# A two-part transformer block with an RWKV-7 chunk loop: b, k and v turned in another way, the block inverse's gather in pieces, GpSimd's order changed

## The chip, the cores and the metric

The kernel runs on one core of one Trainium2 chip, in one launch. The metric is device time in microseconds (us). Five engines work side by side, each through its own list of instructions, in order: TensorE (PE; its weight loads are shown as PEld), VectorE (DVE), ScalarE (ACT), GpSimd (POOL) and SyncE (SP), which here issues transfers. They wait for each other by semaphores only. TensorE writes to PSUM, eight banks of 128 x 512 float32.

## The reference

First two attention blocks with feed-forward parts on 512 tokens of width 1024; then one RWKV-7 block whose core is a recurrence over time for each of 16 heads of width 64, with a state S of 64 x 64:

```python
def step(S, inp):
    r_t, w_t, k_t, v_t, a_t, b_t = inp
    sa = jnp.einsum('bhvk,bhk->bhv', S, a_t)
    S = S * w_t[:, :, None, :] + sa[..., None] * b_t[:, :, None, :] + v_t[..., None] * k_t[:, :, None, :]
    y = jnp.einsum('bhvk,bhk->bhv', S, r_t)
    return S, y
```

Then a norm over each head, a gate, a convolution branch, an output projection and a last feed-forward part. All of it is float32.

## The kernel before

Most of the time goes into projections in which each float32 product is taken as three of rounded halves (lines 2351 to 2353). The change lies in the **chunk loop** between the projections "z" and "rwkv_out". There the recurrence is cut into eight chunks of 64 tokens, taken as four **pairs** j = 0 to 3. Inside a chunk the 64 steps become matrix products that hold the inverse of a triangular 64 x 64 matrix for each head.

The order of the loop is one list, `products` (lines 514 to 533). Each entry is a group of TensorE products with a kind and an index; TensorE, VectorE and ScalarE each walk the list and do what the kind asks. A product takes one of four slots of two PSUM banks in turn (`slot_of`), so TensorE's product m waits until the copies of product m - 4 have been made. Kinds:
- **lab**: b against kk, masked by VectorE into `wk["lab"]`; GpSimd later adds the unit diagonal ("eye", line 964).
- **z, turn, tri, triT**: two levels (4 and 5) that extend the inverse of the 16 x 16 diagonal blocks to 64 x 64. VectorE masks z; ScalarE copies turn and triT. The first level reads `wk["tri"]`, filled by `spread_blocks` (line 599).
- **pairs**: products of b and k with r and kk, masked by VectorE. **v**: v centred and turned, tokens on the partitions. **lv**: its product with `wk["lak"]`.
- **x, u, ys** of chunk i: state against kk; the solve; the output (part 0) and the new state (part 1, which VectorE adds and decays, lines 2192 and 2193).
- **bk** (j, cb) for each chunk cb of pair j: b and k turned so that tokens lie on the partitions, b of the chunk in one half of the 128 partitions and k in the other. One half can be written by a transpose, the other by a product with the identity. ScalarE copies each bank in one go (line 1516). `wk["bk"]` has one buffer for each cb; ys of the state reads it.
- **sums, rows, bonus, rstd**: sums for the head norm.

The inverse of the 16 x 16 blocks works on two pairs at once (a **batch**). `blocks_of` gathers the blocks of both pairs by four operations over 128 x 512 (line 2112), each taking the one before as an input, and turns them (line 2120). `block_inverse` makes 28 small steps, `blocks_back` turns the result into `wk["inv"]` (line 2125), and `spread_blocks` writes a pair's blocks to `wk["tri"]`. Batch 0 (pairs 0 and 1) is VectorE's from gather to spread of pair 0, right behind the masks of lab 1; VectorE masks lab 2 and 3 behind it. Batch 1 (pairs 2 and 3) is gathered by VectorE behind the last pairs mask of pair 0, inverted by GpSimd, and turned back by VectorE behind the last z mask of pair 1. GpSimd's order is: the eyes of lab 0 to 3, those of 2 and 3 only when batch 1 has been gathered, since the gather wants the matrices without them; the inverse of batch 1; the spreads of pairs 1, 2 and 3.

SyncE's queue reloads `u_b` (line 741) with stored activations when the last pairs product and bk (3, 0) are out, then `u_kk` when x 7 is out, then more when ys 7 is.

Of the kernel before, what the change touches and what calls it, by code (L numbers as in the profile page):

```python
# [5 lines left out]
P = 128  # L6
D = 1024
KD = D // P
# [9 lines left out]
C = 64  # L18
# [98 lines left out]
def build(nc, t, out, scratch):  # L117
# [4 lines left out]
    with ctx:  # L122
# [593 lines left out]
        def _(sp):  # L716
# [3 lines left out]
            for p, pan in enumerate(panels):  # L720
# [14 lines left out]
                if p == L["rwkv_out"].p0 + 6:  # L735
# [3 lines left out]
                    product_out(sp, "bk", (NC // 2 - 1, 0))  # L739
# [73 lines left out]
        def _(pool):  # L813
# [186 lines left out]
        def _(act):  # L1000
# [482 lines left out]
            for m, (kind, i) in enumerate(products):  # L1483
                slot = slot_of(m)
                for part in parts_of((kind, i)):
# [22 lines left out]
                    if kind == "v":  # L1508
                        written(act, product, part)
                        for cb in range(2):  # L1510
                            ins = nc.scalar.activation(wk["uv"][side(1 - cb), i % 2, cb, 8 * part:8 * part + 8, :],
                                                       src[side(1 - cb)], ACT.Copy)
                        ins.then_inc(bank_out[bank], 1)
                    if kind == "bk":
                        written(act, product, part)
                        nc.scalar.activation(wk["bk"][:, i[1], 8 * part:8 * part + 8, :], src, ACT.Copy
                                             ).then_inc(bank_out[bank], 1)
# [48 lines left out]
        def _(dve):  # L1566
# [537 lines left out]
            def blocks_of(batch):  # L2104
# [3 lines left out]
                added = masks[:, M_BLOCKS, BS:2 * BS].unsqueeze(1).broadcast_to([P, 2 * RH, BS])  # L2108
                for j in (2 * batch, 2 * batch + 1):
                    product_out(dve, "lab", j)  # L2110
                for q in range(NB):
                    ins = nc.vector.scalar_tensor_tensor(by_row, lab[:, :, q * BS:q * BS + BS], masks[:, M_BLOCKS, q:q + 1],
                                                         added, ALU.mult, ALU.add)
                    if q == NB - 1:
                        ins.then_inc(sg["blocks_read"], 1)
                        dve.wait_ge(sg["blocks_read"], batch + 1)
                    else:
                        link(ins)
                    added = by_row
# [10 lines left out]
            for m, (kind, i) in enumerate(products):  # L2130
                slot = slot_of(m)
                for part in parts_of((kind, i)):
# [3 lines left out]
                    if kind == "lab":  # L2136
# [4 lines left out]
                        if i % 2 and part:  # L2141
                            batch = i // 2
                            if batch == 0:
                                blocks_of(batch)
# [4 lines left out]
                    elif kind == "pairs":  # L2149
# [8 lines left out]
                        if i == (0, 1, 1):  # L2158
                            blocks_of(1)
                    elif kind == "z":  # L2160
# [5 lines left out]
                        if i == (1, LEVELS[1], 1):  # L2166
                            dve.wait_ge(sg["blocks_inverted"], 1)
                            blocks_back(1)
# [21 lines left out]
                    elif kind == "ys" and part == 1:  # L2190
# [3 lines left out]
                                                ALU.mult).then_inc(bank_out[bank], 1)  # L2194

# [81 lines left out]
        def _(pe):  # L2277
# [515 lines left out]
            for m, (kind, i) in enumerate(products):  # L2793
# [23 lines left out]
                elif kind == "v":  # L2817
                    for c in range(KD):
                        dst = ps[:, banks[c // 4], c % 4 * P:(c % 4 + 1) * P]
                        for cb in range(2):  # L2820
                            last = nc.tensor.matmul(dst[side(1 - cb)], u_v[:, c, tokens(i, cb)],
                                                    masks[:, M_CENTER:M_BLOCKS, :].rearrange("p a n -> p (a n)"),
                                                    start=True, stop=True)
                        if c % 4 == 3:
                            last.then_inc(sg["product_done"], 1)
                elif kind == "bk":
                    for c in range(KD):
                        dst = ps[:, banks[c // 4], c % 4 * P:(c % 4 + 1) * P]
# [92 lines left out]
                elif kind == "ys":  # L2921
# [14 lines left out]
                    if 1 in parts_of((kind, i)):  # L2936
                        product_out(pe, "bk", (j, cb))
# [121 lines left out]
```

## Time and profile before

| | us |
|---|---|
| median of 3 timed runs (2365.84 to 2371.52) | 2366.89 |
| the profiled execution | 2364.72 |
| its span, first to last instruction | 2362.8 |
| TensorE busy | 2268.7 (96%) |
| VectorE, ScalarE, GpSimd busy | 1015.0, 875.9, 1024.4 |
| the chunk loop, first lab to last ys on TensorE | 1684.2 to 1856.8 |

Mean granted clock of TensorE over the span: 0.982. In a timeline a row gives start, duration, engine, line, operation, what it writes and reads, the count of instructions merged, and in brackets how long the engine stood idle before it and what ended that. A float32 product counts twice there (two passes), a transpose once. In a table of windows a row gives the stretch and its length, then for each engine its busy time and count, then the granted clock of TensorE as a share of 2.4 GHz (PEclk), the share of the DMA engines and GB/s.

### The profile page before, as it was taken

To read this page: it belongs to the slowest core of one execution; us is meant where nothing else is said; L and a number is where in the kernel's file an instruction comes from. 1 tells how busy PE (TensorE), PEld (TensorE's weight loads), DVE (VectorE), ACT (ScalarE), POOL (GpSimd) and SP (SyncE) were. 2 spreads that over 40 slices of the span, in tenths; PEclk is the share of its full clock that TensorE was granted. 3 is DMA by queue.
4 is the path that set the end of the run, shared out by engine and by line. 5 is a ranking of instruction groups with operands and counts; after the bars stand their busy time and mean duration, and the time that the engine had idled before them with its cause. 6 is when DMAs were issued, how large, how long until landed. Compare 5 with 4: busy or idle time off the path is not lost.

```text
span 2362.8 us, 36049 instructions
## 1 busy us (share of the span) xinstructions
PE 2268.7 (96%) x14668; PEld 1859.4 (79%) x14668; DVE 1015.0 (43%) x1655; ACT 875.9 (37%) x1488; POOL 1024.4 (43%) x605
## 2 busy tenths in 40 slices
PE   7999999999999999999999999999879999999998
PEld 6867888888986688888877888777667778888888
DVE  6264522211456553222125988626843555322212
ACT  5264523322414563332234223353424345333222
POOL 4423544444542264444454444434330465544443
PEclk9999999999999999999999999999979999999999
DMA  6601333333442023333333333322100522333332
GB/s 173 150 23 39 98 106 97 98 96 93 98 119 58 10 72 99 98 98 102 98 86 112 98 99 98 116 94 72 50 3 3 179 77 85 98 99 98 93 98 69
DMA packets 386294, 209.87 MB, mean 89 GB/s; under 512 B 36927, under 2 KB 378663, under 8 KB 385875
## 3 DMA queue, kind: packets, MB, share of 16 engines
q1 hardware_dynamic: 383011, 196.68, 29.4%
q0 software_dynamic: 2448, 9.70, 1.1%
q8 instruction: 119, 1.95, 0.4%
q10 hardware_dynamic: 672, 1.18, 0.1%
q14 instruction: 44, 0.36, 0.0%
HBM read 196.65 MB, written 12.41 MB: 88 GB/s over the span
## 4 chain that ended last, share of the span: by engine, by line
PE 81%; POOL 7%; issue 6%; DVE 4%; ACT 2%; DMA 0%; ACTq 0%; POOLq 0%; DVEq 0%
PE ps L2351 23%; PE ps L2352 23%; PE ps L2353 23%; POOL w_lo L836 3%; PE ps L2561 2%; PE ps L2546 2%; PE ps L2536 2%; POOL x_res L903 1%; PE ps L2831 1%; PE ps L2524 1%; POOL u_b L933 0%; PE ps L2933 0%; PE ps L2885 0%; PE ps L2814 0%; PE ps L2424 0%
## 5 line engine op out<-in xcount | busy, mean ns | idle before, releaser
L836 POOL TENSOR_TENSOR w_lo<-raw,w_hi 128x1024 fp32r<-128x1024 f32 (+2 forms) x344 | 823.2, 2397 | 887.2 <-ACT w_hi L1025 882.2
L2351 PE MATMUL ps<-h_hi,w_hi 128*128 128x512 f32 (+1 forms) x2112 | 817.5, 387 | 20.5 <-DVE h_lo L1712 4.5
L2352 PE MATMUL ps<-h_hi,w_lo 128*128 128x512 f32 (+1 forms) x2112 | 805.3, 381 | 0.0
L2353 PE MATMUL ps<-h_lo,w_hi 128*128 128x512 f32 (+1 forms) x2112 | 805.2, 381 | 0.0
L1025 ACT ACTIVATE w_hi<-raw 128x1024 fp32r<-128x1024 f32 (+1 forms) x344 | 358.6, 1043 | 1113.4 <-PE ps L2353 1101.7
L2351 PEld LDWEIGHTS ps<-h_hi,w_hi 128*128 128x128 f32 x2112 | 399.3, 189 | 113.5 <-issue 31.7
L2353 PEld LDWEIGHTS ps<-h_lo,w_hi 128*128 128x128 f32 x2112 | 399.3, 189 | 77.1
L2352 PEld LDWEIGHTS ps<-h_hi,w_lo 128*128 128x128 f32 x2112 | 399.7, 189 | 74.7 <-issue 1.2
L2351 PE MATMUL ps<-hid_hi,w_hi 128*128 128x512 f32 (+1 forms) x616 | 221.8, 360 | 0.0
L2353 PE MATMUL ps<-hid_lo,w_hi 128*128 128x512 f32 (+1 forms) x616 | 220.9, 359 | 0.0
L2352 PE MATMUL ps<-hid_hi,w_lo 128*128 128x512 f32 (+1 forms) x616 | 220.9, 359 | 0.0
L1991 DVE SCALAR_TENSOR_TENSOR ps<-u_w,vecs,ps 128x511 f32<-128x511 f32 (+28 forms) x232 | 151.9, 735 | 0.0
L1776 DVE TENSOR_TENSOR hid<-ps,spread_s 128x512 f32<-128x512 f32 x66 | 45.6, 691 | 242.5 <-PE ps L2353 242.5
L1770 DVE TENSOR_TENSOR silu<-ps,spread_s 128x512 f32<-128x512 f32 x66 | 45.6, 691 | 229.3 <-PE ps L2353 229.2
L1594 DVE TENSOR_TENSOR h_sq<-h_sq 128x512 f32<-128x512 f32 x16 | 36.1, 2259 | 248.2 <-ACT h_sq L1130 157.0
L2352 PEld LDWEIGHTS ps<-hid_hi,w_lo 128*128 128x128 f32 x616 | 116.4, 189 | 17.2
L2353 PEld LDWEIGHTS ps<-hid_lo,w_hi 128*128 128x128 f32 x616 | 116.3, 189 | 17.3
L2351 PEld LDWEIGHTS ps<-hid_hi,w_hi 128*128 128x128 f32 x616 | 116.3, 189 | 17.1
L873 POOL TENSOR_TENSOR h_lo<-o_raw,h_hi 128x512 fp32r<-128x512 f32 x16 | 20.4, 1276 | 88.5 <-ACT h_hi L1240 88.5
L1260 ACT ACTIVATE score<-score,row_max 128x257 f32<-128x257 f32 (+3 forms) x96 | 49.7, 519 | 19.9 <-DVE row_max L1825 17.6
L1764 DVE TENSOR_TENSOR hid_lo<-hid,hid_hi 128x512 fp32r<-128x512 f32 x66 | 53.8, 816 | 2.9 <-ACT hid_hi L1203 2.6
L1203 ACT ACTIVATE hid_hi<-hid 128x512 fp32r<-128x512 f32 x66 | 41.9, 635 | 34.9 <-DVE hid L1780 34.9
(359 smaller groups left out, 2508.7 us busy)
## 6 DMA issues: line engine op xcount, KB each, us to landing
raw<-in_w_gu SPq DMA_DIRECT2D x88, 512.0 KB, 3.8
raw<-in_w_in SPq DMA_DIRECT2D x56, 512.0 KB, 3.9
raw<-in_w_down SPq DMA_DIRECT2D x32, 448.0 KB, 3.5
raw<-in_ffn_w_gate SPq DMA_DIRECT2D x22, 512.0 KB, 3.9
raw<-in_ffn_w_up SPq DMA_DIRECT2D x22, 512.0 KB, 3.8
raw<-in_w_in_b SPq DMA_DIRECT2D x20, 512.0 KB, 3.8
raw<-in_w_down SPq DMA_DIRECT2D x16, 512.0 KB, 3.8
raw<-in_w_out SPq DMA_DIRECT2D x16, 512.0 KB, 3.7
```

Of the source, the lines that this page charges most:

```text
L836: nc.gpsimd.tensor_tensor(lo[:, k0:, :], src[:, k0:, :], hi[:, k0:, :].bitcast(f32), ALU.subtract).then_inc(lo_done, 1)
L1025: nc.scalar.activation(w_hi[split_slot[p]][:, k0:pan.kc, :], raw[:, raw_slot[p], k0:pan.kc, :], ACT.Copy).then_inc(hi_done, 1)
L1260: nc.scalar.activation(score[:, b, 0:w], score[:, b, 0:w], ACT.Exp, scale=-1.0, bias=row_max[:, b:b + 1], accum_out=total).then_inc(sg["ex ...
L1764: nc.vector.tensor_tensor(hid_lo[:, f, :], hid[:, f % 2, :], hid_hi[:, f, :].bitcast(f32), ALU.subtract).then_inc(sg["hid_lo_ready"], 1)
L1770: nc.vector.tensor_tensor(silu[:, f % 2, :], ps[:, g % 4, :], spread_s[:, :], ALU.mult).then_inc(bank_free[g % 4], 1)
L1991: nc.vector.scalar_tensor_tensor(u_kk[:, c, s:TOK] if last else acc[:, s:TOK], u_w[:, c, 0:TOK - s], tap(TAPS - 1 - s, c), acc[:, s:TOK], ...
L2351: nc.tensor.matmul(bank, wh[:, k, :], ah[:, part], start=first, stop=False)
L2352: nc.tensor.matmul(bank, wl[:, k, :], ah[:, part], start=False, stop=False)
L2353: return nc.tensor.matmul(bank, wh[:, k, :], al[:, part], start=False, stop=end)
L2536: nc.tensor.matmul(ps[:, i % 4, 0:u["w"]], u["q"], u["k"], start=True, stop=True).then_inc(sg["s_done"], 1)
L2546: last = nc.tensor.transpose(ps[0:m, 4 + k % 2, j * P:(j + 1) * P], score[:, k % SCORE_BUFFERS, off:off + m], ident[:, :])
L2561: ins = nc.tensor.matmul(ps[side(e), 6 + tile % 2, blk * P:(blk + 1) * P], v, pT[0:m, (k + e) % PT_BUFFERS, j * P:(j + 1) * P], start=(j = ...
```

## The change

1. **b and k.** The kinds bT j and kT j take the place of bk (j, cb). Each is eight whole 128 x 128 transposes, both chunks of the pair at once. In the result the tokens of each chunk fill one half of the partitions; ScalarE copies b straight and k into the other half of the partitions, each bank in two copies of 64 partitions. Pair 0 has both where the bk products were; for j > 0, bT, lv, kT stand behind the odd ys (and sums), none behind the even ys.
2. **v.** Products of 64 x 64 by the two diagonal blocks of the centring matrix, all heads of one parity to one bank.
3. **The gather of batch 1** is made in four pieces behind z (0, 5, 1), x 0 and z (1, 4, 0), from the matrices that have their eyes already, and turned behind z (1, 4, 1). `blocks_back(1)` stands behind ys 1.
4. **GpSimd** adds the eyes of lab 2 and 3 at once, and spreads pair 1 ahead of the inverse of batch 1.
5. SyncE's reload of `u_b` waits for bT 3.

```diff
-                products += [("lab", 0), ("lab", 1), ("v", 0), ("bk", (0, 0)), ("bk", (0, 1)), ("lab", 2), ("lab", 3)]
+                products += [("lab", 0), ("lab", 1), ("v", 0), ("bT", 0), ("kT", 0), ("lab", 2), ("lab", 3)]
...
-                products += [x0] + first + [u0] + pairs0 + middle + [ys0, ("bk", (j, 0))] + last + [x1] + pairs1 + [u1]
+                products += [x0] + first + [u0] + pairs0 + middle + [ys0] + last + [x1] + pairs1 + [u1]
...
-                products += [("bk", (j, 1))] if j < NC // 2 - 1 else []
-                products += [("lv", j)]
+                products += [("bT", j), ("lv", j), ("kT", j)]
...
-                    product_out(sp, "bk", (NC // 2 - 1, 0))
+                    product_out(sp, "bT", NC // 2 - 1)
...
                 product_out(pool, "lab", j)
-                pool.wait_ge(sg["blocks_read"], j // 2 + 1)
+                if j < 2:
+                    pool.wait_ge(sg["blocks_read"], 1)
...
-            pool.wait_ge(sg["blocks_turned"], 2)
-            block_inverse(nc.gpsimd, link).then_inc(sg["blocks_inverted"], 1)
             for j in range(1, NC // 2):
+                if j == 2:
+                    pool.wait_ge(sg["blocks_turned"], 2)
+                    block_inverse(nc.gpsimd, link).then_inc(sg["blocks_inverted"], 1)
                 pool.wait_ge(sg["blocks_back"], j // 2 + 1)
                 written(pool, ("turn", (j - 1, LEVELS[0], 1)))
                 spread_blocks(nc.gpsimd, j).then_inc(sg["tri_first"], 1)
...
+                            ins = nc.scalar.activation(wk["uv"][side(1 - cb), i % 2, cb, part::2, :], src[side(1 - cb)], ACT.Copy)
...
+                        for cb in range(2):
+                            to = side(cb if kind == "bT" else 1 - cb)
+                            ins = nc.scalar.activation(wk["bk"][to, cb, 8 * part:8 * part + 8, :], src[side(cb)], ACT.Copy)
...
+                    if batch:
+                        dve.wait_ge(sg["lab_eye"], 8)
+                        link(nc.vector.tensor_scalar(by_row, block, chosen, None, ALU.mult))
+                        return
...
+            def beside(product):
+
+                if product == ("z", (0, LEVELS[1], 1)):
+                    gather(1, 0)
+                    gather(1, 1)
+                if product == ("x", 0):
+                    gather(1, 2)
+                if product == ("z", (1, LEVELS[0], 0)):
+                    gather(1, 3)
+                if product == ("z", (1, LEVELS[0], 1)):
+                    turn_blocks(1)
+                if product == ("ys", 1):
+                    dve.wait_ge(sg["blocks_inverted"], 1)
+                    blocks_back(1)
...
                     for c in range(KD):
+                        for e in range(2):
+                            center = masks[side(e), M_CENTER + e, :]
+                            for cb in range(2):
+                                last = nc.tensor.matmul(ps[side(1 - cb), banks[e], c * C:(c + 1) * C],
+                                                        u_v[side(e), c, tokens(i, cb)], center, start=True, stop=True)
...
-                        for src, block in ((u_b, i[1]), (u_k, 1 - i[1])):
-                            turn = nc.tensor.matmul if block else nc.tensor.transpose
-                            last = turn(dst[side(block)], src[:, c, tokens(*i)], ident[:, :])
+                        both = (u_b if kind == "bT" else u_k)[:, c, 2 * i * C:(2 * i + 2) * C]
+                        last = nc.tensor.transpose(ps[:, banks[c // 4], c % 4 * P:(c % 4 + 1) * P], both, ident[:, :])
```

ys of the state (part 1) waits for bT j and kT j where it waited for bk (j, cb).

## Rows read from the trace of the kernel before

**Rows 1.** The page's part 4: the chain that ended last, by engine.

```profile
PE 81%; POOL 7%; issue 6%; DVE 4%; ACT 2%; DMA 0%; ACTq 0%; POOLq 0%; DVEq 0%
```

**Rows 2.** Timeline of TensorE, chunk pairs 0 and 1.

```profile
1699.04 2.09 PE L2804 MATMUL ps<-u_rkk,u_b 64*64 64x64 f32 x128
...
1709.65 1.13 PE L2885 MATMUL ps<-wk_tri,wk_lab 64*64 64x64 f32 x32 [8.52 <-DVE wk_tri L599]
...
1721.17 0.46 PE L2897 MATMUL ps<-ident,wk_tri 64*128 64x64 f32 x8 [0.50 <-DVE wk_lak L2156]
...
1727.08 1.98 PE L2870 MATMUL ps<-wk_uv,wk_lak 64*64 64x64 f32 x64 [5.45 <-DVE wk_z L2163]
...
1728.85 3.52 PE L2918 MATMUL ps<-wk_triT,wk_z 64*64 64x64 f32 x62
...
1744.41 1.13 PE L2885 MATMUL ps<-wk_tri,wk_lab 64*64 64x64 f32 x32 [11.30 <-POOL wk_tri L599]
```

**Rows 3.** Timeline of VectorE, the same stretch and the masks behind.

```profile
1721.04 1.09 DVE L2112 SCALAR_TENSOR_TENSOR wk_cols<-wk_lab,masks 128x512 f32<-128x512 f32 x1
...
1722.17 3.39 DVE L2112 SCALAR_TENSOR_TENSOR wk_cols<-wk_lab,masks,wk_cols 128x512 f32<-128x512 f32 x3
...
1726.34 1.29 DVE L2163 TENSOR_TENSOR wk_z<-ps,masks 128x512 f32<-128x512 f32 x2
...
1762.73 1.14 DVE L2125 STREAM_TRANSPOSE wk_inv<-wk_rows 128x512 f32<-128x512 f32 x1
```

**Rows 4.** Timeline of GpSimd: eyes, first step of the inverse, spread.

```profile
1725.72 4.96 POOL L964 TENSOR_TENSOR wk_lab<-wk_lab,masks 128x512 f32<-128x512 f32 x4 [25.46 <-DVE wk_cols L2112]
...
1730.65 0.27 POOL L589 TENSOR_TENSOR step_of<-wk_rows 128x28 f32<-128x28 f32 x1
...
1742.38 1.89 POOL L599 TENSOR_TENSOR wk_tri<-wk_inv,masks 128x1024 f32<-128x1024 f32 x1
```

**Rows 5.** Windows; PE busy first, PEclk after the POOL column.

```profile
1715.60:1721.60 6.00, 5.43 (x224) 4.87 (x218) 5.88 (x10) 1.20 (x2) 0.00 (x0) 0.99 0.02 4
1727.10:1732.70 5.60, 5.60 (x150) 5.60 (x153) 0.52 (x1) 1.86 (x4) 5.21 (x9) 0.50 0.01 3
1744.40:1749.80 5.40, 5.39 (x122) 4.93 (x126) 1.38 (x2) 1.22 (x3) 0.00 (x0) 0.50 0.01 3
1749.80:1778.60 28.80, 28.75 (x767) 23.20 (x761) 11.59 (x17) 12.29 (x22) 1.89 (x1) 1.00 0.01 4
```

**Rows 6.** Timeline of TensorE, later pairs.

```profile
1755.60 0.30 PE L2831 MATMUL ps<-ident,u_b 128*64 128x128 f32 x1
...
1755.83 0.43 PE L2831 MATMUL ps<-ident,u_k 128*64 128x128 f32 x2
...
1760.34 0.69 PE L2885 MATMUL ps<-wk_tri,wk_lab 64*64 64x64 f32 x32
...
1765.57 2.07 PE L2918 MATMUL ps<-wk_triT,wk_z 64*64 64x64 f32 x62
...
1767.57 1.97 PE L2821 MATMUL ps<-masks,u_v 128*64 128x128 f32 x32
...
1806.88 1.95 PE L2965 MATMUL ps<-head_ones,u_k 128*128 128x2 f32 x16
```

**Rows 7.** Timeline of TensorE: the transposes of x_in.

```profile
35.81 3.86 PE L2650 MATMUL ps<-ident,x_in 128*128 128x128 f32 x32 [0.78 <-issue]
```

**Rows 8.** Window of line 2650 alone: PE, PEld, PEclk, DMA share, GB/s.

```profile
35.80:39.40 3.60, 3.59 (x32) 3.39 (x32) 1.00 0.62 134
```

**Rows 9.** Timeline of ScalarE: copies of v, a copy of bk.

```profile
1768.71 2.42 ACT L1511 ACTIVATE wk_uv<-ps 64x512 f32<-64x512 f32 x4 [0.43 <-PE ps L2821]
...
1774.90 0.60 ACT L1516 ACTIVATE wk_bk<-ps 128x512 f32<-128x512 f32 x1 [2.06 <-PE ps L2831]
```

**Rows 10.** Line 741, the reload of u_b.

```profile
L741 SPq DMA_DIRECT2D u_b<-scratch_conv x8: 432/435/1387, 1835.0 to 1840.1; - x8
DMA to landing us min/median/max: 4.3/5.7/6.4
```

More of the change, by code:

```diff
@@ L1510, in _ @@
                         for cb in range(2):
-                            ins = nc.scalar.activation(wk["uv"][side(1 - cb), i % 2, cb, 8 * part:8 * part + 8, :],
-                                                       src[side(1 - cb)], ACT.Copy)
+                            ins = nc.scalar.activation(wk["uv"][side(1 - cb), i % 2, cb, part::2, :], src[side(1 - cb)], ACT.Copy)
                         ins.then_inc(bank_out[bank], 1)
-                    if kind == "bk":
+                    if kind in ("bT", "kT"):
                         written(act, product, part)
-                        nc.scalar.activation(wk["bk"][:, i[1], 8 * part:8 * part + 8, :], src, ACT.Copy
-                                             ).then_inc(bank_out[bank], 1)
+                        for cb in range(2):
+                            to = side(cb if kind == "bT" else 1 - cb)
+                            ins = nc.scalar.activation(wk["bk"][to, cb, 8 * part:8 * part + 8, :], src[side(cb)], ACT.Copy)
+                        ins.then_inc(bank_out[bank], 1)
                     if kind == "lv":
@@ L2102, in mask4, with gather @@
                 return m.broadcast_to([m.shape[0], 2, 4, C])
-            def blocks_of(batch):
+            def gather(batch, q):
                 lab = wk["lab"][:, 2 * batch:2 * batch + 2, :, :].rearrange("p j h n -> p (j h) n")
                 by_row = wk["cols"][:, :, :, :].rearrange("p t j h -> p (j h) t")
[L2108 to L2119, printed above, removed]
+                block, chosen = lab[:, :, q * BS:q * BS + BS], masks[:, M_BLOCKS, q:q + 1]
+                if q == 0:
+                    for j in (2 * batch, 2 * batch + 1):
+                        product_out(dve, "lab", j)
+                    if batch:
+                        dve.wait_ge(sg["lab_eye"], 8)
+                        link(nc.vector.tensor_scalar(by_row, block, chosen, None, ALU.mult))
+                        return
+                added = by_row if q else masks[:, M_BLOCKS, BS:2 * BS].unsqueeze(1).broadcast_to([P, 2 * RH, BS])
+                ins = nc.vector.scalar_tensor_tensor(by_row, block, chosen, added, ALU.mult, ALU.add)
+                if q == NB - 1:
+                    ins.then_inc(sg["blocks_read"], 1)
+                    dve.wait_ge(sg["blocks_read"], batch + 1)
+                else:
+                    link(ins)
@@ L2120, in blocks_of, with turn_blocks @@
+            def turn_blocks(batch):
                 nc.vector.transpose(wk["rows"][:, :, :, :], wk["cols"][:, :, :, :]).then_inc(sg["blocks_turned"], 1)
                 dve.wait_ge(sg["blocks_turned"], batch + 1)
+            def beside(product):
[11 more added lines that the diff above has]
+                    blocks_back(1)
@@ L2143, in _ @@
                             if batch == 0:
-                                blocks_of(batch)
+                                for q in range(NB):
+                                    gather(batch, q)
+                                turn_blocks(batch)
                                 link(block_inverse(nc.vector, link))
@@ L2157, in _ @@
                                                 ).then_inc(bank_out[bank], 1)
-                        if i == (0, 1, 1):
-                            blocks_of(1)
                     elif kind == "z":
@@ L2165, in _ @@
                                                 mask(M_LOW + l - LEVELS[0], [P, 2, 4, C]), ALU.mult).then_inc(bank_out[bank], 1)
-                        if i == (1, LEVELS[1], 1):
-                            dve.wait_ge(sg["blocks_inverted"], 1)
-                            blocks_back(1)
                     elif kind == "tri" and i[1] == 0:
@@ L2194, in _ @@
                                                 ALU.mult).then_inc(bank_out[bank], 1)
+                beside((kind, i))
             def low_of_y(c):
@@ L2818, in _ @@
                     for c in range(KD):
[L2819 to L2826, printed above, removed]
+                        for e in range(2):
[3 more added lines that the diff above has]
+                                                        u_v[side(e), c, tokens(i, cb)], center, start=True, stop=True)
+                            if c == KD - 1:
+                                last.then_inc(sg["product_done"], 1)
+                elif kind in ("bT", "kT"):
                     for c in range(KD):
-                        dst = ps[:, banks[c // 4], c % 4 * P:(c % 4 + 1) * P]
-                        for src, block in ((u_b, i[1]), (u_k, 1 - i[1])):
-                            turn = nc.tensor.matmul if block else nc.tensor.transpose
-                            last = turn(dst[side(block)], src[:, c, tokens(*i)], ident[:, :])
+                        both = (u_b if kind == "bT" else u_k)[:, c, 2 * i * C:(2 * i + 2) * C]
+                        last = nc.tensor.transpose(ps[:, banks[c // 4], c % 4 * P:(c % 4 + 1) * P], both, ident[:, :])
                         if c % 4 == 3:
@@ L2936, in _ @@
                     if 1 in parts_of((kind, i)):
-                        product_out(pe, "bk", (j, cb))
+                        product_out(pe, "bT", j)
+                        product_out(pe, "kT", j)
                         for h in range(RH):
```

## The prediction

> **What bounds the kernel now.** I began with the page: the span is 2362.8 us, and TensorE has 81% of the chain of work that ended last [rows 1]. So what the change is worth is what it takes from TensorE's line inside the chunk loop, and only the places count at which TensorE waits or is itself late. Second came the timeline of TensorE through the loop, read for the brackets of idle time [rows 2]. There are three large ones. At 1709.65 it has waited 8.52 us for VectorE's first wk_tri, at 1727.08 5.45 us for VectorE's z, and at 1744.41 11.30 us for GpSimd's wk_tri. Third, the timelines of the two engines named. VectorE stands in `blocks_of(1)`, four gathers (1.09 + 3.39) and a transpose, from 1721.04, and only at 1726.34 masks the z for which TensorE waits [rows 3]. GpSimd adds the eyes of chunk pairs 2 and 3 only after that gather (4.96 us from 1725.72), then runs the 28 steps of the block inverse from 1730.65 to 1742.4, and only then, for 1.89 us, spreads the blocks of pair 1, which it had in hand all the time (they come from batch 0) [rows 4]. Fourth, the same stretch in windows: the granted clock is 0.99 while TensorE works in 1715.6 to 1721.6, and 0.50 in the 5.6 us of work that follow its stand; it is 0.50 again in the 5.4 us after the long wait, and 1.00 for the 28.8 us behind that, in which TensorE is busy for 28.75 [rows 5]. So from 1755 on no wait is left: TensorE's own products are the time, and there every product taken away counts in full until another engine is late.
>
> **The change part by part.**
> *The first wait (8.52 us) stays.* It ends with VectorE's own inverse of batch 0, whose gathers, transposes and steps are as before. The shorter v and the transposes that stand before it only lengthen TensorE's idle time. So z of pair 0 starts at 1709.65 as before. Value 0; it could move by some tenths only if the masks of lab 0 and 1 moved, which nothing here touches.
>
> *The second wait (5.45) goes.* With the gather out of the way, VectorE masks z right behind the last pairs mask, at 1721.1; a mask takes 0.69, of which 0.6 up to the next start. lv of pair 0 needs the bank of the first z, so it starts at about 1721.85 in place of 1727.08: 5.2 us. What is late next is nothing of VectorE's: gather pieces 0 and 1 (2 x 1.1) stand behind the z masks, from 1722.4 to 1724.6, and x 0 reaches VectorE later than that.
>
> *The third wait (11.30) goes.* POOL's order is now eyes 0 and 1, eyes 2 and 3, spread 1, inverse, spread 2. Lab 2 and 3 are out at 1711.9, so the eyes end near 1716; spread 1 needs the last turn of pair 0, which ends at 1721.6 [rows 2], and is done 1.89 later, at 1723.6. x 0 ends at 1725.6 (next term), so z of pair 1 doesn't wait: 11.3 us. The inverse (11.75 us with its steps' gaps [rows 4]) starts when VectorE has turned the blocks, at about 1731, and ends near 1743; VectorE asks for it after the state update of ys 1, near 1750. It has 7 us to spare.
>
> *The clock between them.* lv and triT of pair 0 took 1.98 and 3.52 us at the half clock (1.2 GHz) [rows 2]; triT takes 2.07 at the full one (2.4 GHz) [rows 6], a factor of 1.7, by which lv takes 1.2: 2.3 us. TensorE no longer stands before them, so I take the full clock; the low end is 0. Behind the long wait TensorE worked 5.4 us at 0.50 [rows 5]; a z took 1.13 us there [rows 2] and 0.69 at the full clock [rows 6], a factor of 1.6, so this becomes 3.3: another 2.1 us.
>
> *bk by whole transposes.* Before, one bk product took 4.7 us from its first start to the next product (1755.60 to 1760.34; the other in the pair is its mirror image): per 128 columns a transpose of 64 tokens (0.23 us to the next start) and a plain product of two passes (the other 0.36 of 0.59) [rows 6]. There is no whole transpose in the loop; the nearest row is the 32 of x_in, 128 x 128 each, all of whose starts lie within 3.60 us at granted clock 1.00: 0.113 us each [rows 7, 8]. A bT or kT product is eight of them, 0.9 us. Bounds: 0.9 by that row, 1.8 if each went at the pace of the 64-token transpose in the loop (0.23); I take 0.9, since it is the same form. Pairs 1 and 2 had two bk products and get two short ones: 9.4 - 1.8 = 7.6 us each. Pair 3 had one bk and gets two short ones: 2.9. Pair 0 lies before the first wait: 0. Sum 18.1 us.
>
> *v by 64x64 products.* 1.97 us busy before, 1.9 to the next start [rows 6]. The new form (32 products in four quadrants, 64 moving columns) is that of lab, of which two went in 2.09 us [rows 2]: 1.0. Three v products count (pairs 1 to 3): 2.7 us.
>
> *What is added.* Gross this makes 5.2 + 11.3 + 2.3 + 2.1 + 18.1 + 2.7 = 41.7 us. Against it stand new waits, since three engines now have less time for the same copies.
> (a) Pair 1: VectorE has gather pieces 2 and 3 (2 x 1.1) and the turn (0.7) between x 0 and the masks of the pairs. Placed one by one behind x 0 (ends 1726.3), they push the last pairs mask from about 1731.5 to 1733.3, and ys 0 behind it: 1.8 us.
> (b) Behind each ys of odd number now stand bT, lv and kT on TensorE, 0.9 + 1.2 + 0.9. ScalarE must copy 4 + 2 + 4 times, where it copied 2 + 2; a copy over 64 partitions costs as much as one over 128 (4 in 2.42 us, against 0.60 for one) [rows 9]. The PSUM bank pair of a product is taken again four products later, so the second z of the next pair waits for kT's copies. Before pair 2: kT is out 6.4 us behind the end of ys, TensorE would be there at 5.0, and z waits 0.9 before that for the spread that comes behind `blocks_back` (two operations on the state, each as long as a mask, 1.4; blocks_back 1.1 [rows 3]; spread 1.89 [rows 4]): together 1.6 us. Before pair 3 there is also sums (1.95 us on TensorE [rows 6], two copies): kT is out at 8.4, TensorE there at 6.8: 1.6 us. In the tail the second sums waits 0.4 in the same way.
> The copies of kT cross from one half of the partitions to the other, and no row shows such a copy on ScalarE: between 0.60, as in [rows 9], and twice that. I take 0.60; at 1.2 the waits grow by 2.4 us at each of three places, 7 us.
> (c) The reload of u_b on SP's queue waits for bT 3 in place of bk (3, 0), so it starts near the end of pair 3 and not at 1835. Its eight pieces are issued in 5.1 us and each lands within 6.4 of its issue [rows 10]; the next transfer in the queue waits for x 7, 11 us later. It stays hidden; without that cover it would cost up to its 12 us.
> New waits 1.8 + 1.6 + 1.6 + 0.4 = 5.4. In these TensorE stands up to 1.6 us at a place, and before, it lost the full clock after standing; for one such fall I put in what the first one cost, 2.3 us. Net 41.7 - 5.4 - 2.3 = 34.0 us.
>
> The profiled execution took 2364.72 us (span 2362.8 and 1.9 around it), so the sum says 2330.7. The median of the three timed runs is 2.2 above the profiled one; the forecast for the median is 2333 us.
>
> **The rivals.**
> *The clock falls at every joint.* Behind ys now come sums, two products of nothing but transposes and a wait, where bk had kept TensorE going for 4.7 us. For it speaks that the clock was 0.50 after each stand in [rows 5]; against it, that 32 whole transposes in a row ran at 1.00 [rows 7, 8]. Work from bT to the second turn is 5.8 us at the full clock and 9.9 at the half one (factor 1.7), but the wait of 1.6 is then covered: 2.5 us; u, pairs and tri behind it cost 2 more. At three joints 13 us, gain 21 to 23: 2344 us.
> The Trainium skill, in "TensorE: Matmul & The Clock Gate", Part 4 (PE-mode transpose), says that the full clock does not engage for transposes. By it this rival would be the likely one; the x_in transposes, 0.113 us apart at granted clock 1.00, do not agree with it.
> *No new waits.* ScalarE's and VectorE's copies overlap better than I stack them. In [rows 9] two 64-partition copies never started less than 0.6 apart, which speaks against. Gain 41: 2326 us.
> *Copies across the halves are slow:* 1.2 us each, gain 27: 2340 us.
> *The waits only move.* The inverse on GpSimd runs beside a busy VectorE now, where before VectorE had nothing to do, and VectorE is blocked in order behind `blocks_inverted`. It decides from an inverse of 19 us (now 11.75); at 35 us the gain is down to 18: 2349 us. Against it: two of VectorE's masks took 1.29 us right beside GpSimd's adds, and those kept to 1.24 each [rows 3, 4].
> *Slower.* The clock stays at 1.2 GHz from 1722 to the end of the loop: dense small products and transposes do not bring it back as bk did. Some 100 us of TensorE work remain there, at 1.6 to 1.7 times the time: +60, against 36 gained: 2390 us. It decides from some 55 us of the loop at the half clock. Against it: between 1749.8 and 1778.6 the same small products ran at 1.00, bk being 9.4 of the 28.8 us [rows 5].
>
> **How the numbers follow.** Forecast (gain 28 to 38) 0.60; clock at every joint 0.17; no new waits 0.08; slow copies 0.08; waits only moved 0.04; slower 0.03. Range: from 2324 (all of 41.7 and a little) to 2346 (the clock rival and a little). Less than 0.3%, 7 us, cannot be told from no change in this kernel; half of the moved-waits case lies there. Faster 0.95, the same 0.02, slower 0.03.
>
> **What would show it.** TensorE starts lv of pair 0 near 1722, and z of pair 1 near 1726 without a wait for wk_tri. bT and kT are 8 transposes each, 0.9 us a product; v 1.0 us. ScalarE's copies behind odd ys are ten or twelve in a row, and the second z of pairs 2 and 3 waits for them. x 2 ends about 27 us earlier than 1778.8, the loop about 34 to 36 us earlier. The prediction is wrong if the granted clock of the loop is below 0.8 over long stretches, if VectorE waits for `blocks_inverted`, if a whole transpose takes more than 0.2 us, or if ScalarE becomes the engine that never waits in the loop.

## The result, and the profile after

| | before | after |
|---|---|---|
| median of the timed runs, us | 2366.98 (4 runs) | 2335.44 (2332.80 to 2337.06, 4 runs) |
| the profiled execution, its span, us | 2364.72, 2362.8 | 2332.80, 2331.0 |
| mean granted clock of TensorE | 0.982 | 0.986 |

The ratio is 0.9862, interval 0.9845 to 0.9879. The forecast was 2333 (2324 to 2346). In the page, TensorE's share of the chain that ended last is as before; GpSimd's has fallen by 1% of the span, and "issue" has grown by 1% [rows 1]:

```profile
PE 81%; issue 7%; POOL 6%; DVE 4%; ACT 2%; DMA 0%; ACTq 0%; POOLq 0%; DVEq 0%
```

To see where the time went I cut the loop where a product starts on TensorE. Each column runs from one such start to the next ("z 0" is the first z of pair 0, "z 1" that of pair 1). The last column ends at the last start among those products of ys 7 that read the state (1863.82 before, 1833.55 after), so this loop is longer than the one that the table of the kernel before gives (to 1856.8):

| us | lab 0 to z 0 | to lv 0 | to z 1 | to x 2 | to x 4 | to x 6 | to ys 7 | loop |
|---|---|---|---|---|---|---|---|---|
| before | 25.42 | 17.43 | 17.33 | 33.73 | 36.33 | 32.33 | 17.02 | 179.58 |
| after | 25.38 | 12.11 | 4.74 | 27.55 | 30.76 | 31.58 | 18.42 | 150.52 |
| taken away | 0.0 | 5.3 | 12.6 | 6.2 | 5.6 | 0.8 | -1.4 | 29.1 |
| by the prediction | 0 | 5.2 | 13.6 | 8.8 | 6.9 | 2.2 | -0.4 | 36.3 |

The last line is the prediction's own terms put in their places, without its 2.3 us for a fall of the clock that had no place. Between the two profiled executions lie 31.9 us: 29.1 in the loop, 1.2 in an earlier start of it, 1.6 behind it. Those 2.9 us are in no step. The loop starts at 1682.4 to 1690.6 in executions whose instructions are the same up to there, so single executions are compared below by the loop alone. The loop varies too: a second profiled execution of the changed kernel (h_after, below) has 151.60 us in place of 150.52.

TensorE's timeline of the changed kernel; [rows 2, 6] have the same products of before:

```profile
1708.40 1.13 PE L2904 MATMUL ps<-wk_tri,wk_lab 64*64 64x64 f32 x32 [16.22 <-DVE wk_tri L598]
...
1720.52 1.16 PE L2889 MATMUL ps<-wk_uv,wk_lak 64*64 64x64 f32 x64
...
1723.66 1.29 PE L2937 MATMUL ps<-wk_triT,wk_z 64*64 64x64 f32 x30 [1.05 <-issue]
...
1725.31 0.66 PE L2904 MATMUL ps<-wk_tri,wk_lab 64*64 64x64 f32 x30
...
1749.66 1.09 PE L2850 MATMUL ps<-ident,u_b 128*128 128x128 f32 x8
1750.68 1.16 PE L2889 MATMUL ps<-wk_uv,wk_lak 64*64 64x64 f32 x64
1751.78 1.09 PE L2850 MATMUL ps<-ident,u_k 128*128 128x128 f32 x8
...
1754.36 0.69 PE L2904 MATMUL ps<-wk_tri,wk_lab 64*64 64x64 f32 x32 [0.86 <-POOL wk_tri L598]
...
1756.42 0.69 PE L2904 MATMUL ps<-wk_tri,wk_lab 64*64 64x64 f32 x32 [0.97 <-issue]
...
1787.17 0.69 PE L2904 MATMUL ps<-wk_tri,wk_lab 64*64 64x64 f32 x32 [1.97 <-issue]
```

The reader is to see four things. The first wait ends where it did, with more idle time in it. The waits of 5.45 and 11.30 us are gone. Eight whole transposes stand where a bk product of 4.7 us did. And new small waits stand before the first z of pair 2 (the spread) and the second z of pairs 2 and 3, where "issue" hides ScalarE, whose copies fill the time without a gap:

```profile
1750.35 2.42 ACT L1518 ACTIVATE wk_bk<-ps 64x512 f32<-64x512 f32 x4 [0.42 <-PE ps L2850]
1752.80 1.08 ACT L1522 ACTIVATE wk_xx<-ps 128x512 f32<-128x512 f32 x2
1753.90 2.42 ACT L1518 ACTIVATE wk_bk<-ps 64x512 f32<-64x512 f32 x4
```

The last of these copies ends at 1756.32, and the second z starts at 1756.42. Windows of the changed kernel, columns as in [rows 5]: from the first z, over pairs 0 and 1, and the tail.

```profile
1708.40:1714.40 6.00, 6.00 (x137) 5.53 (x138) 4.13 (x7) 1.19 (x2) 4.80 (x4) 0.50 0.01 3
1714.40:1752.80 38.40, 33.19 (x1231) 30.31 (x1226) 25.90 (x36) 17.32 (x31) 12.72 (x31) 1.00 0.02 5
...
1815.10:1833.50 18.40, 17.53 (x293) 15.01 (x294) 7.78 (x14) 7.82 (x18) 7.29 (x5) 0.81 0.48 154
```

After the first wait the clock is at 0.50 (1.2 GHz) for 6 us as before, and then it holds 1.00 through three pairs. But in the second window TensorE is busy for only 33.19 of 38.40 us, although the timeline shows one wait for a semaphore in it, of 0.50 us. Seven rows with idle time and no releaser (0.33 to 1.05 us, two of them in the fences here: 1723.66 and 1746.87) make up 4.4 of the other 4.7. That gap is the part that the prediction had no term for, although the trace of before has such rows too, between 1778 and 1840 us:

```profile
1781.09 0.57 PE L2885 MATMUL ps<-wk_tri,wk_lab 64*64 64x64 f32 x21 [1.02 <-issue]
...
1789.01 0.33 PE L2933 MATMUL ps<-wk_mrbk,wk_uv 128*64 128x64 f32 x3 [0.97 <-issue]
...
1838.87 0.88 PE L2821 MATMUL ps<-masks,u_v 128*64 128x128 f32 x12 [1.71 <-issue]
```

### The profile page after: what moved, and what is told of

Read it like the earlier page. It is cut to its first block, busy times and chain, and to the rows that moved or that the text cites. A ratio compares the mean times of both kernels' runs of the same rounds, so it can differ in the third digit from the quotient of the medians.

```text
span 2331.0 us, 36126 instructions
## 1 busy us (share of the span) xinstructions
PE 2232.4 (96%) x14692; PEld 1838.9 (79%) x14692; DVE 1015.4 (44%) x1655; ACT 885.3 (38%) x1506; POOL 1024.3 (44%) x605
## 3 DMA queue, kind: packets, MB, share of 16 engines
q8 instruction: 119, 1.95, 0.3%
## 4 chain that ended last, share of the span: by engine, by line
PE 81%; issue 7%; POOL 6%; DVE 4%; ACT 2%; DMA 0%; ACTq 0%; POOLq 0%; DVEq 0%
PE ps L2372 23%; PE ps L2374 23%; PE ps L2373 23%; POOL w_lo L835 3%; PE ps L2582 2%; PE ps L2567 2%; PE ps L2557 2%; POOL x_res L902 1%; PE ps L2545 1%; POOL u_b L932 0%; PE ps L2952 0%; PE ps L2835 0%; PE ps L2946 0%; PE ps L2445 0%; POOL scratch_z L943 0%
```

## The experiments

### Which part brings what: f_order, f_turns, f_v_old

f_order is the kernel before with parts 3 and 4 of the change alone (VectorE's pieces, GpSimd's order). f_turns is the kernel before with parts 1 and 5 alone (bT and kT). f_v_old is the changed kernel with the old v:

```diff
 # f_v_old, against the changed kernel (TensorE; ScalarE's copies as before, too)
-                            center = masks[side(e), M_CENTER + e, :]
-                            for cb in range(2):
-                                last = nc.tensor.matmul(ps[side(1 - cb), banks[e], c * C:(c + 1) * C],
-                                                        u_v[side(e), c, tokens(i, cb)], center, start=True, stop=True)
+                        (the v product of the kernel before: 128 rows by 128 columns, 64 tokens)
```

> The kernel before with the gather in pieces and GpSimd's new order alone; bk and v as before. By my terms: the waits of 5.45 and 11.30 us go, the half clock after them goes (2.3 + 2.1), and the gather pieces push ys 0 by 1.8: gain 19 us, near 2348. The rival (the waits were worth little, since bk and v behind them were the bound) says under 8 us. Second question: in the changed kernel TensorE stands 0.6 to 1.3 us at every 131st weight load, where no semaphore is late. If that is the fetch of its instructions, which slow bk products let run ahead, then here, with bk kept, few of these stand beside those of before (3 of over 1 us in pairs 1 to 3).

> The kernel before with bT and kT alone; gather, GpSimd's order and v as before. By my terms: bk gives 7.6 + 7.6 + 2.9 = 18.1, and the waits for ScalarE's copies take 0.7 + 1.6 + 0.4 back: gain 15 us. If standing at each 131st weight load is the price of faster products (instruction fetch), 3 to 5 us less: gain 10 to 12, near 2356. The long waits of 5.45 and 11.30 stay as they are. Rival: bT and kT are hidden by other waits, gain under 5.

> The changed kernel with v in its old form (16 products of 128 x 64 by 128 columns). By my term the loop is longer by 0.9 at each of three v, 2.7 us. By the fetch theory less, 0 to 2 us: the new form has twice the instructions (64 weight loads against 32), so its gain is partly paid back by one stand more in each pair of two.

| | us, runs | ratio to before | loop of the profiled execution |
|---|---|---|---|
| f_order | 2353.44, 4 | 0.9938 (0.9920 to 0.9956) | 163.47 |
| f_turns | 2353.33, 4 | 0.9934 (0.9916 to 0.9952) | 169.44 |
| f_v_old | 2339.12, 1 | | 155.38 |

By the ratios the order is worth 14.7 us and the turns 15.6, each give or take 4; together 30.3 of the 32.7 that the ratio of the whole change stands for. Within that noise the parts add up. What is left for v, 2.4 (predicted 2.7), is smaller than the noise and does not size it. In f_order the two waits are gone as in the changed kernel (12.12 and 4.75 us in the second and third column). Its shortfall against the 19 expected has a visible part: from x 2 to x 4 it is 2.5 us slower than before, and there the clock had fallen.

```profile
1793.20:1803.40 10.20, 10.20 (x153) 6.42 (x153) 0.66 (x2) 2.28 (x4) 0.00 (x0) 0.50 0.01 2
```

In f_turns the long waits stay (17.42, 17.27) and pairs 1 and 2 shrink as in the changed kernel (27.86, 30.23). Its profiled execution was its slowest (2361.86), so its loop says less than its ratio. f_v_old's loop is 4.9 us longer than the changed kernel's, more than either side had expected; it has one place at which TensorE stands for 3.40 us and three falls of the clock that the other has not, so a single execution does not size v either. What v brings was not measured.

### What makes TensorE stand: f_shift

A **stand** is a place in the loop at which more than 0.4 us lie between the starts of two weight loads, with no semaphore wait at the second one (the 512-column products and those slowed by the half clock, whose own pace is over 0.4 us, are left out). In the trace I numbered the entries of TensorE's weight-load queue from the start of the program; semaphore waits stand in it as entries too. The stands are not spread by kind of product. In the changed kernel they come at entry 10099, 10231, 10363, 10495, 10626, 10757, 10887, ..., 11677, 11808, ..., 12597, 12728: at distances of 130 to 132 entries (124 to 126 weight loads), in whatever product that is. The count becomes exact when products are counted too. If all that TensorE runs is counted, weight loads, products and semaphore waits, the number of entries ahead of a stand leaves 193 or 194 when divided by 256; this holds for all 120 stands in the loops of the twelve profiled executions. In the loop before there are 3 stands, 4.5 us together; in the changed kernel 13, 12.8 us. (Each has one more at the same count, 0.48 and 0.44 us, where a semaphore wait falls on it.) f_order has 6, 6.2 us, and f_turns 4, 5.6 us: each part of the change alone leaves most of them away, and both together bring them. The change did not take instructions away. The loop has 7784 entries after it, 7728 before, in 29 us less.

One theory: they belong to the position in the instruction stream, so they are the fetching of instructions. The rival: they are hidden waits for other engines, which belong to the product. In the expectations "weight load 10099" is this entry 10099, and "every 131st weight load" this distance. f_shift puts 66 weight loads (33 products of two passes) into the first wait, which costs no time there:

```diff
+                    # f_shift, before the first z of pair 0
+                    for _ in range(33):
+                        nc.tensor.matmul(ps[:, banks[0], 0:C], ident[:, :], ident[:, 0:C], start=True, stop=True)
```

> The changed kernel with 33 small products (66 weight loads and 66 matmuls, results unused) put into TensorE's first long wait, before z of pair 0, where they cost nothing. Fetch theory: TensorE stands 0.6 to 1.3 us at the same counts of weight loads from the start (10099, 10231, 10363, 10495, ...), which are now other products, 66 weight loads earlier in the list; the total stays within 1.5 us. Rival (a semaphore, a bank or a copy is late): it stands in the same products as before, at counts 66 higher.

The time is 2334.39 us (one run), the loop 148.82. The 10 stands (9.8 us) lie on the same series of counts, to within two (10493, 10755, 10886, 11017, 11807, 12596, 12727 among them), and so in other products. Entry 10887 of the changed kernel stood in ys 1, behind eleven products of it; in f_shift entry 10886 is a v product, earlier in the list. The changed kernel, then f_shift:

```profile
1746.87 0.85 PE L2946 MATMUL ps<-u_rkk,state 64*64 64x64 f32 x21 [0.71 <-issue]
```

```profile
1745.42 1.04 PE L2846 MATMUL ps<-masks,u_v 64*64 64x64 f32 x54 [0.68 <-issue]
```

The rival of hidden waits falls. That it is the fetch is argued from the transfers. Beside the bulk data there is a queue that carries instructions, q8, with 119 packets and 1.95 MB over the whole span, 16.4 KB each. In 1732 to 1736 us it moves one:

```profile
q8 instruction: 1, 0.02, 1.4%
```

Three things tie this queue to the stands. First, the numbers agree: TensorE runs 30270 entries in f_turns and f_v_old, 30526 in the changed kernel and 30658 in f_shift, and q8 has 118, 119 and 120 packets there, one for each 256 entries to within one packet. Second, the time: all 120 stands end 2.2 to 3.1 us behind the start of a q8 packet, whether that packet started before the stand or up to 0.95 us into it (packet at 1733.30, stand 1734.53 to 1735.71; packet at 1744.54, stand 1745.88 to 1746.86). Third, the rate: in no loop do two packets start less than 3.3 us apart, and where one stand follows another, from 1723 to 1747 us, they come 3.5 to 4.3 us apart. In the window 1714.4 to 1752.8 the changed kernel runs 256 entries in 3.9 us on average; before, in the dense stretch 1749.8 to 1778.6, they took 4.8, and there was no stand. No run changed the size of the program's pieces. That a stand is tied to the count and to the packet is shown; that the packet holds the instructions TensorE lacks is inferred from these three.

### Waits and their neighbours: g_clock, g_copies, g_early, g_loads

These four start from the changed kernel and ran once each, on one chip with each other and not with h_after. Their times are not read as gains: the loops of two executions of the changed kernel differ by 1.1 us. What is read are columns and waits that repeat.

```diff
 # g_clock: TensorE works through the last part of the first wait
+                    for _ in range(12):
+                        nc.tensor.matmul(ps[:, banks[0], :], ident[:, :], vecs[:, 0:512], start=True, stop=True)
 # g_copies: VectorE takes the second bank of each bT and kT
-                    if kind in ("bT", "kT"):                     (ScalarE)
+                    if kind in ("bT", "kT") and part == 0:       (ScalarE)
+                    elif kind in ("bT", "kT") and part == 1:     (VectorE, tensor_copy)
 # g_early: VectorE turns the blocks back ahead of ys 1, behind the last pairs mask
-                if product == ("ys", 1):
+                if product == ("pairs", (1, 1, 1)):
 # g_loads: SyncE's loads of w_rwkv_out wait for ys 5, not for the last z mask
-                    written(sp, ("z", (NC // 2 - 1, LEVELS[1], 1)))
+                    written(sp, ("ys", NC - 3), 1)
```

> The changed kernel with 12 fill products of 512 columns (results unused) in TensorE's long first wait, so that the clock is up when z of pair 0 starts. If the half clock behind that wait is a cost on the path: z, turn and the first pairs of pair 0 take 1.7 times less, VectorE's idle 1.83 before the first pairs mask goes, and z of pair 0 to lv of pair 0 takes 10.4 in place of 12.1 us. If VectorE's masks alone set that stretch: under 0.5 us. If the fills run past the end of VectorE's inverse, the first stretch (25.4 us) grows by what they run over.

> The changed kernel with the second bank of each bT and kT copied by VectorE, so ScalarE has 2 + 2 + 2 copies behind an odd ys in place of 4 + 2 + 4. By my terms the second z of pairs 2 and 3 no longer waits for a bank (0.97 and 1.97 us) nor the second sums in the tail (0.36): 3 us less; the wait of 0.86 for the spread of pair 2 stays. If each such wait was also time in which TensorE's instructions were fetched, half of it comes back as stands at other counts: 1.5 us. Rival (ScalarE was not what they waited for): no change.

> The changed kernel with blocks_back of batch 1 behind the last pairs mask of pair 1 (GpSimd's inverse has ended 1 us before) in place of behind ys 1. The wait of 0.86 us for wk_tri before z of pair 2 goes; but the second z then waits that much longer for kT's copies: 0.97 becomes about 1.8, and the total stays within 0.3 us. Rival: the two waits were independent, 0.9 us less.

> The changed kernel with the four loads of w_rwkv_out, now issued behind the last z of pair 3, issued behind ys 5. In all kernels so far TensorE stands longest at one count of weight loads (12728, or 12600 with the old v): 1.7 to 3.4 us, right behind these four loads. If instruction fetch stands behind their packets, it is now about 1.0 us there, and pair 3's stretch is 0.9 us shorter; the next such count lies among sums and bT, slow enough to hide it. Rival: the stand belongs to the place in the program and stays 1.9 or more.

| us | one run | lab 0 to z 0 | to lv 0 | to z 1 | to x 2 | to x 4 | to x 6 | to ys 7 | loop |
|---|---|---|---|---|---|---|---|---|---|
| g_clock | 2339.18 | 25.68 | 11.31 | 3.60 | 27.19 | 31.48 | 33.67 | 17.20 | 150.13 |
| g_copies | 2335.65 | 26.66 | 13.58 | 4.73 | 26.40 | 29.40 | 32.69 | 16.15 | 149.63 |
| g_early | 2338.13 | 25.62 | 12.11 | 4.74 | 27.00 | 31.41 | 32.19 | 15.68 | 148.75 |
| g_loads | 2329.21 | 25.50 | 12.11 | 3.27 | 27.21 | 30.73 | 31.81 | 17.03 | 147.66 |

**g_clock** gave part of what it should: z 0 to lv 0 is 0.8 us shorter, where the full clock would give 1.7. Its fillers ended 6.8 us before z 0, and the clock was at 0.50 again from 1709.8 to 1716.6.

**g_early** took away the wait of 0.86 us for the spread. The second z of pair 2 then waited for 1.98 us in place of 0.97:

```profile
1760.82 0.69 PE L2904 MATMUL ps<-wk_tri,wk_lab 64*64 64x64 f32 x32 [1.98 <-issue]
```

So the two are one wait: ScalarE's copies of kT end when they end, and whatever makes TensorE arrive earlier is given back there.

**g_copies** took those away (the second z of pair 2 follows the first at once, and x 2 to x 4 is 1.4 us shorter). It lost as much at the start: VectorE's copies for pair 0 stand behind its own inverse, z 0 waits for their bank, and the first two columns are 2.8 us longer.

**g_loads** took on the longest stand of the loop, at entry 12728, in the v of pair 3. In the changed kernel four loads of 512 KB run beside it, at 87% of the DMA engines' time from 1797 to 1806 us; the stand takes 1.9 us from one weight load to the next. The changed kernel, then g_loads:

```profile
1805.64 0.57 PE L2843 MATMUL ps<-masks,u_v 64*64 64x64 f32 x22 [1.65 <-issue]
```

```profile
1803.53 0.57 PE L2843 MATMUL ps<-masks,u_v 64*64 64x64 f32 x22 [0.55 <-issue]
```

Same product, same count, same 22 records behind it. In the ten profiled executions that keep the loads there, this stand took 1.7 to 3.4 us; in the two with the loads moved (g_loads, h_best), 0.8 and 0.7. The q8 packet itself comes later beside them: 5.1 us after the one before in the changed kernel, 4.1 in g_loads. A bulk transfer beside it makes a stand longer. The rest of the 2.9 us by which this loop is shorter than the changed kernel's goes with fewer stands (10, 9.4 us) and cannot be told from what single executions differ by.

### All four together: h_best, beside h_after

h_best has 19 fillers, g_early, g_loads, and g_copies with pair 0 left to ScalarE. h_after is the changed kernel once more, on the same chip.

```diff
-                    for _ in range(12):
+                    for _ in range(19):
-                    if kind in ("bT", "kT") and part == 0:
+                    if kind in ("bT", "kT") and (part == 0 or i == 0):
-                    elif kind in ("bT", "kT") and part == 1:
+                    elif kind in ("bT", "kT") and part == 1 and i:
```

> The changed kernel with four edits: 19 fill products in TensorE's first wait (so that they end shortly before z of pair 0 and the clock does not fall), the second bank of bT and kT copied by VectorE for pairs 1 to 3 (for pair 0 by ScalarE, since VectorE stands in the inverse there), blocks_back of batch 1 behind the last pairs mask of pair 1, and the loads of w_rwkv_out behind ys 5. By what the runs gave singly: 1.8 us from the clock, 3.3 from the three waits for kT's copies, 0.9 from the spread, 1.1 from the loads; the stands for instruction fetch stay: 6 to 7 us under the changed kernel, near 2329, ratio to the kernel before 0.983 to 0.984. Rival (each wait taken away comes back as a fetch stand or a fallen clock): under 2 us.

> The changed kernel once more, beside the former on the same chip. Both theories: ratio to the kernel before 0.985 to 0.988; stands at the weight-load counts 10099 and every 131 or 132 behind it as in its first profile, falls of the clock at other places.

| us | median, 4 runs each | ratio to before | z 0 to lv 0 | x 2 to x 4 | x 4 to x 6 | loop |
|---|---|---|---|---|---|---|
| h_after | 2334.98 | 0.9864 (0.9847 to 0.9880) | 12.11 | 30.88 | 33.65 | 151.60 |
| h_best | 2327.82 (2326.53 to 2330.67) | 0.9837 (0.9823 to 0.9852) | 10.61 | 29.92 | 29.11 | 144.09 |

h_after repeats the result: 2334.98 against 2335.44. h_best is 7.2 us faster than h_after, 7.5 by the loops; no run of one reaches the runs of the other. That is what the four were to give together (6 to 7), and the rival of under 2 us falls. How the 7.5 divide is not shown: the profiled execution of h_after has a fall of the clock of 3.4 us in the column x 4 to x 6 and h_best has none, and the stands from z 0 on are 14, 13.5 us, against 12, 10.5. The fillers now last up to z 0, and the clock stays up. Windows of h_best, up to z 0 and from there to lv 0:

```profile
1684.00:1709.90 25.90, 25.35 (x374) 15.51 (x374) 22.35 (x45) 8.49 (x14) 7.74 (x6) 0.93 0.10 32
1709.90:1720.60 10.70, 9.41 (x357) 8.20 (x356) 9.96 (x17) 2.51 (x5) 4.99 (x5) 1.00 0.02 5
```

## Why the prediction was right, and what it lacked

- **The first wait stays: right.** 25.38 us from lab 0 to z 0 against 25.42.
- **The second wait goes: right**, 5.3 us for 5.2. The z masks now stand right behind those of the pairs, and the gather behind them. VectorE, then GpSimd:

```profile
1719.79 1.27 DVE L2186 TENSOR_TENSOR wk_z<-ps,masks 128x512 f32<-128x512 f32 x2
1720.98 1.90 DVE L2116 TENSOR_SCALAR wk_cols<-wk_lab,masks 128x512 f32<-128x512 f32 x1
1722.92 1.11 DVE L2119 SCALAR_TENSOR_TENSOR wk_cols<-wk_lab,masks,wk_cols 128x512 f32<-128x512 f32 x1
```

```profile
1720.54 1.89 POOL L598 TENSOR_TENSOR wk_tri<-wk_inv,masks 128x1024 f32<-128x1024 f32 x1 [5.97 <-PE ps L2916]
...
1730.55 0.28 POOL L588 TENSOR_TENSOR step_of<-wk_rows 128x28 f32<-128x28 f32 x1 [8.12 <-DVE wk_rows L2128]
...
1742.61 0.24 POOL L590 TENSOR_TENSOR wk_rows<-wk_rows,step_of 128x28 f32<-128x28 f32 x1
```

- **The third wait goes: right in kind, 12.6 us for 13.6.** The spread is done at 1722.43 and z of pair 1 starts at 1725.25, with no wait for it. The inverse takes 12.3 us (11.75 before) and ends at 1742.85; VectorE turns it back behind ys 1, at 1751.11, so the 7 us to spare held, and "the waits only move" did not come. The missing 1 us is the stand of 1.05 inside triT.
- **The turns: right.** A bT or kT takes 1.02 us up to the next start, for 0.9; v about 1.1, for 1.0. Over six short products and three v that is 1 us. ScalarE's copies across the halves cost the same 0.6 as others, as taken: eight of them in 2 x 2.42 us.
- **The new waits: three of four right in place and size.** Before pair 2 0.86 and 0.97 us, together 1.8 for 1.6; before pair 3 1.97 for 1.6; tail 0.36 for 0.4. That both of pair 2 are one wait, ended by kT's copies, g_early and g_copies have shown. The fourth, 1.8 us in pair 1 for the gather pieces, was not paid: the last pairs mask ends at 1733.33, as forecast, but ys 0 does not stand behind it and starts at 1732.49, and no product of pair 1 waits for a semaphore. Whether it would have waited without the stands ahead of it, no run shows. TensorE, then VectorE:

```profile
1732.49 1.11 PE L2946 MATMUL ps<-u_rkk,state 64*64 64x64 f32 x32
```

```profile
1732.64 0.69 DVE L2181 TENSOR_TENSOR wk_lak<-ps,masks 64x512 f32<-64x512 f32 x1
```

- **The reload of u_b: right.** It is issued at 1815.19, the next transfer of the queue at 1830.08 behind x 7, and no product of the loop waits for either.
- **The clock: better than feared.** The two terms for the full clock behind the waits that went (2.3 and 2.1) came: the granted clock is 1.00 from 1714.4 on. No fall in pairs 1 to 3 of the profiled execution, where 2.3 us were set aside; one in the tail of 6.8 us (1820.2 to 1827.0) against 3.4 before, which is the 1.4 us by which the last column grew. Other kernels had falls of 3.4 to 10.2 us in the middle pairs, at differing places; "the clock falls at every joint" is not what any trace shows.
- **Transposes and the clock.** The rule of the Trainium skill ("TensorE: Matmul & The Clock Gate", Part 4) that the full clock does not engage for transposes is again not borne out: bT and kT ran in 1.02 us at granted clock 1.00, with lv between them. They are short and stand among products that had the clock up; what a long stretch of transposes alone does to it, no run here shows.
- **What failed: the sum assumed that TensorE's products, with no wait left, run end to end.** "Every product taken away counts in full until another engine is late" left out the stands at fixed counts, three of which stood in the trace of before. They went from 4.5 to 12.8 us. By column they grew by 1.3 (to z 1), 5.0 (to x 2), 0.8 (to x 4) and 1.2 (to x 6). These 8.3 us, 1.0 in the tail (1.4 where 0.4 was forecast) and 1.0 for the turns are 10.3. Against them stand the 1.8 of pair 1 that were not paid. That leaves 8.5, where 7.2 lie between 36.3 and 29.1: the account closes to 1.3 us. The old bk products and waits had given the instruction stream time (4.8 us for 256 entries behind the long wait); the new, denser products use up 256 entries in 3.9 us, and then TensorE goes at the pace of the packets. The median still came out 2.4 us from the forecast, since the 2.3 set aside for the clock and the 2.9 outside the loop stood against the missing term: the mechanism was right, the closeness is in part luck. The prediction's own signs say the same: x 2 was to end 27 us earlier and ended 25.3 earlier, the loop 34 to 36 and was 30.3.

## What to carry to other kernels

When the last waits of a stretch of many small products are taken away, count TensorE's instructions per microsecond as well, weight loads, products and semaphore waits together: where 256 of them took 3.9 us on average the engine stood between its own instructions, and where they took 4.8 it did not. An average can hide a dense spot (before, 1778.1 to 1814.5 us: 5.0 on average, and two stands), so look also for rows with idle time and no releaser in the trace of before. Keep bulk loads away from such a stretch, since four of them lengthened the stand beside them. Fill a wait that cannot be removed with work for TensorE up to its very end if the products behind it pay for the clock: fillers that ended 6.8 us early gave 0.8 us, those that lasted gave 1.5 (12.11 to 10.61). A small wait behind another is often the same one: look which copy ends last before you remove the first.

## What was not expected of the hardware

- The stands: 0.4 to 1.7 us each, one at most for each 256 instructions of TensorE counted from the program's start, where small products follow closely; 1.7 to 3.4 us beside 512 KB loads.
- VectorE's first gather (a TENSOR_SCALAR) took 1.90 us beside GpSimd's spread (1720.54 to 1722.43), the ones behind it 1.11; those are another operation, so the difference is not the price. In all ten profiled executions with this order the first gather began 0.45 us behind the start of the spread. It took 1.90 to 2.18 us, as the spread took 1.89 to 2.17, and it ended 0.45 to 0.48 us behind the spread's end in each. Other TENSOR_SCALAR operations of 128 x 512 from SBUF to SBUF took 0.53 to 0.54. "SBUF — State Buffer" of the Trainium skill (SBUF: two separate sides) says that the two engines share a pair of ports for which one waits while the other's instruction runs. The trace agrees: the gather looks held until the spread was done. The masks that read PSUM did not slow down beside GpSimd (two in 1.27).
- The clock's falls come at differing places in kernels with nearly the same products (1793 in f_order, 1820 after), and one of 10.2 us costs some 4 us of an execution (by the factor of 1.6 of [rows 2, 6]); a gain of that size in a single execution shows nothing.
